# One decoder layer with expert retrieval: GpSimd takes part in the one-hot batches, the last table store goes in three parts, and the first group's roots are multiplied in behind its projections

## What is computed

```python
xn = rmsnorm(h, norm_mix_g);  proj = xn @ w_in               # 2048 columns: a | b | c | v
ya = rmsnorm(pool_mixer(a), norm_a_g)                        # windows 2, 4, 8, 16, then a 128x128 map
yb = rmsnorm(b * causal_conv3(c * v), norm_b_g)
h  = (h + concat(ya, yb) @ w_out)[16:]
xf = rmsnorm(h, norm_ffn_g)
s  = (xf @ w_query) . sub_keys                               # 8 heads, 2 halves, 128 keys each
top 16 of each half -> 256 sums -> top 16 -> expert = 128*i1 + i2, gates = softmax
out = h + sum over 8*16 experts of gate * gelu(u_e . xf) * v_e;  out = rmsnorm(out) * g
```

## Time and profile before

| | us |
|---|---|
| median of 3 runs | 2589.92 |
| the profiled execution, its own time | 2585.36 |
| its span | 2583.3 |
| PE busy | 2485.5 (96%) |
| DVE busy | 1967.7 (76%) |
| POOL busy | 1438.9 (56%) |
| ACT busy | 430.4 (17%) |
| mean granted clock of PE | 0.988 |

### The profile page before, as it was taken

One profiled execution on the slowest core, in us unless ns is written; L12 is line 12 of the kernel. 1 busy time (PEld: TensorE's weight loads), 2 busy tenths in 40 slices (PEclk: granted clock), 3 DMA queues, 4 the chain that ended last, 5 costly groups with the idle time before them and its releaser, 6 DMA issues.

```text
span 2583.3 us, 23989 instructions
## 1 busy us (share of the span) xinstructions
PE 2485.5 (96%) x7573; PEld 1367.0 (53%) x7573; DVE 1967.7 (76%) x4240; ACT 430.4 (17%) x793; POOL 1438.9 (56%) x1169
## 2 busy tenths in 40 slices
PE   8999999999788899999999999999999999999998
PEld 6687785877666344444444444444444444444443
DVE  3308888788699779676888868778787777979788
ACT  1213313213787000010020000000000000000001
POOL 0000387587611257556666757666676766767664
PEclk9999999999999999999999999999999999999999
DMA  7553885865678889969999999999999999999997
GB/s 291 220 185 142 306 302 148 347 207 132 204 229 240 340 317 373 399 244 418 371 394 390 389 405 371 410 378 414 414 386 419 360 397 413 405 420 403 419 405 275
DMA packets 288061, 857.67 MB, mean 332 GB/s; under 512 B 42048, under 2 KB 99392, under 8 KB 273344
## 3 DMA queue, kind: packets, MB, share of 16 engines
q0 software_dynamic: 167184, 541.73, 55.4%
q1 hardware_dynamic: 108400, 289.25, 29.5%
q10 hardware_dynamic: 12352, 25.17, 2.6%
HBM read 807.75 MB, written 48.30 MB: 331 GB/s over the span
## 4 chain that ended last, share of the span: by engine, by line
PE 70%; POOL 8%; DMA 8%; DVE 5%; issue 4%; ACT 3%; DVEq 1%; ACTq 0%; SPq 0%
PE pairs L820 27%; PE pairs L774 27%; PE pairs L684 9%; DMA ring<-in_expert_u,idx 6%; POOL gate_tables L635 5%; POOL ring L664 4%; PE pairs L731 2%; PE pairs L706 2%; ACT arena L972 1%; PE pairs L787 1%; DVE junk L1173 1%; ACT pick_all L853 1%; DMA arena<-gate_tables 1%; DMA arena<-in_w_all 1%; ACT arena L996 1%
## 5 line engine op out<-in xcount | busy, mean ns | idle before, releaser
L664 POOL DMA_INDIRECT ring<-in_expert_u,idx x512 | 645.1, 1260 | 644.0 <-DVE dots L1173 391.1
L820 PE MATMUL pairs<-arena 128*128 128x512 f32 x2048 | 887.3, 595 | 14.7 <-DVE arena L1239 8.5
L774 PE MATMUL pairs<-arena 128*128 128x512 f32 x2048 | 882.5, 592 | 0.0
L1173 DVE CUSTOM_DVE_ANT_0 junk<-ring,xf 128x1024 bf16<-128x1024 f32 x512 | 612.8, 1223 | 196.0 <-DMA ring<-in_expert_u,idx 192.2
L664 POOL DMA_INDIRECT ring<-in_expert_v,idx x512 | 576.8, 1127 | 293.5 <-DVE arena L1184 134.1
L820 PEld LDWEIGHTS pairs<-arena 128*128 128x128 f32 x2048 | 390.4, 191 | 509.1 <-issue 501.3
L774 PEld LDWEIGHTS pairs<-arena 128*128 128x128 f32 x2048 | 388.6, 190 | 486.5 <-issue 486.5
L1184 DVE SCALAR_TENSOR_TENSOR arena<-ring,arena 128x1024 f32<-128x1024 f32 x381 | 474.3, 1281 | 107.5 <-DMA ring<-in_expert_v,idx 106.4
L684 PE MATMUL pairs<-arena 128*128 128x256 f32 (+1 forms) x1792 | 397.4, 385 | 9.0 <-ACT arena L927 5.3
L684 PEld LDWEIGHTS pairs<-arena 128*128 128x128 f32 x1792 | 344.0, 192 | 60.4 <-ACT arena L927 5.9
L980 ACT ACTIVATE arena<-pairs 128x512 f32<-128x512 f32 x128 | 76.3, 597 | 1177.5 <-PE pairs L774 1159.9
(11 more groups left out here) (169 smaller groups left out, 1093.8 us busy)
## 6 DMA issues: line engine op xcount, KB each, us to landing
arena<-in_w_all SPq DMA_DIRECT2D x80, 1024.0 KB, 6.4
arena<-in_uT SPq DMA_DIRECT2D x128, 512.0 KB, 7.8
arena<-in_expert_v SPq DMA_DIRECT2D x128, 512.0 KB, 9.6
arena<-gate_tables SPq DMA_DIRECT2D x32, 1024.0 KB, 9.1
gate_tables<-arena SPq DMA_DIRECT2D x11, 2048.0 KB, 9.7
gate_tables<-junk ACTq DMA_DIRECT2D x4, 2048.0 KB, 15.1
ring<-in_expert_u,idx POOLq DMA_INDIRECT x512, 9.2
ring<-in_expert_v,idx POOLq DMA_INDIRECT x512, 8.8
```

The costliest lines, as they stand in the source:

```text
L664: nc.gpsimd.indirect_dma_start(out=ring[:, r % RING, :], out_offset=None, in_=expert_u if table == "u" else expert_v, in_offset=bass.Indir ...
L774: last = nc.tensor.matmul(score_bank[x], uslot[:, x % USLOTS, k * P:(k + 1) * P], xfT[:, k, :], start=(k == 0), stop=(k == KD - 1))
L820: last = nc.tensor.matmul(o_bank[n % 4], gated[:, x % GSLOTS, t * P:(t + 1) * P], vrows[:, j, half * 512:(half + 1) * 512], start=(j == 0) ...
L1173: nc.vector.tensor_tensor_reduce(out=junk[:, r % 2, :], in0=row, in1=xf[:, t % 2, :], scale=1.0, scalar=0.0, op0=ALU.mult, op1=ALU.add, ac ...
```

## The change

The first group's columns are multiplied by the gain alone, ahead of everything (`tensor_scalar`, in place). `pa` step 0 runs ahead of `sumsq`. The squares are added up on DVE first (`add_x(0)`), so that `sumsq` has two matmuls in place of eight. The reciprocal root, kept in `work` and not in `std`, is multiplied in when DVE evicts the ten `pa` and `bcv` steps of group 0 (`scaled`); ACT evicts none of these.

In the batches, ACT makes the first one-hots of batch 1 and of batches 2, 6, 10, ... (13), DVE those of 0, 4, 8, ... (12), and POOL those of 3, 5, 7, ..., 47 (23), by eight `tensor_scalar` of 128x128 each. In POOL's queue they stand ahead of the gather that follows the row used by batch b-3 plus the ring: batch 3 ahead of the gather of row 72, batches 5 and 7 ahead of row 73, and so on. The last store is in three parts, and the gates 1 wait for the second part and no longer for the whole.

`FILL` has a new place y2 between `add_y` and `roots_y`, and other figures. By the planner, 28 and 29 rows are used in the two queries, 27 and 28 before, and the scatters stand behind the gathers of rows 35 and 64.

```diff
-        for gate, y, outp, query in ((0.0, 0.0, 0.0, 0.0), (4.0, 22.0, 10.0, 68.0), (4.0, 22.0, 10.0, 68.0), (0.0, 15.0, 0.0, 66.0))]
+        for gate, y, y2, outp, query in ((0.0, 0.0, 0.0, 0.0, 0.0), (4.0, 13.0, 6.0, 10.0, 70.0), (4.0, 13.0, 6.0, 10.0, 70.0), (0.0, 10.0, 3.0, 0.0, 66.0))]
...
-    steps = [("sumsq", 0, 0)] + [("pa", 0, i) for i in range(4)]
+    steps = [("pa", 0, 0), ("sumsq", 0, 0)] + [("pa", 0, i) for i in range(1, 4)]
...
+    evictor = [{"outp": "dve", "ynorm": "roots"}.get(kind, "dve" if n == 0 and kind in ("pa", "bcv") else "act") for kind, n, _ in steps]
...
+                    "gate": ("bcv", n, 5), "y": ("pool", n, 0) if n < GRPS - 1 else ("turn", n, GT - 1), "y2": ("outp", n, GT - 1), "outp": ("ynorm", n, 0)}[where]
...
+        BY_ACT = [b for b in range(BATCHES) if b == 1 or b % 4 == 2]
+        BY_POOL = [b for b in range(BATCHES) if b % 2 == 1 and b > 1]
+        rows_then = [rows + sum(len(plan["hots", c]) for c in range(b + 1)) - sum(len(plan["hots", c]) for c in range(BATCHES)) for b in range(BATCHES)]
+        hots_before = {}
+        for b in BY_POOL:
+            hots_before.setdefault(rows_then[b - 3] + RING, []).append(b)
...
-                    sp.dma_start(to[:, 2:], of[:, 2:]).then_inc(table_kept[c % STAGES], 16)
+                    sp.dma_start(to[:, 2:HALF_GROUPS // 2], of[:, 2:HALF_GROUPS // 2]).then_inc(next_kept, 16)
+                    sp.dma_start(to[:, HALF_GROUPS // 2:], of[:, HALF_GROUPS // 2:]).then_inc(table_kept[c % STAGES], 16)
...
+            sp.wait_ge(next_kept, 16)
+            load_gates(1)
             stage_kept(last_stage)
-            load_gates(1)
...
+            def first_hots(b):
+                c = b % HOTBUFS
+                pool.wait_ge(table_full, 2 * (b - HOTBUFS) + 2)
+                if b // (P // HOTS) > 0:
+                    pool.wait_ge(turned_out, b // (P // HOTS))
+                for t in range(HOTS):
+                    k = b * HOTS + t
+                    last = nc.gpsimd.tensor_scalar(hots[:, c, 0, t, :], iota[:], routeT[:, 0, k:k + 1], None, ALU.is_equal)
+                last.then_inc(hot_pool, 1)
...
+                    for b in hots_before.get(r, ()):
+                        first_hots(b)
...
-                if b % 2 == 1:
-                    pe.wait_ge(hot_first, b // 2 + 1)
+                if b in BY_ACT:
+                    pe.wait_ge(hot_act, BY_ACT.index(b) + 1)
+                elif b in BY_POOL:
+                    pe.wait_ge(hot_pool, BY_POOL.index(b) + 1)
...
+            def scaled(kind, i):
+                step = (kind, 0, i)
+                dve.wait_ge(pe_step, full(step))
+                pair = psum[:, position[step] % PAIRS, :]
+                if kind == "pa":
+                    nc.vector.tensor_tensor(abuf[0][:, i, :], pair[:, 0:COLS], root_x(0), ALU.mult).then_inc(dve_emptied, 1)
+                else:
+                    halves = pair.rearrange("p (c t) -> p c t", c=2)[:, :, 0:COLS]
+                    nc.vector.tensor_tensor(projb[:, 2 * i:2 * i + 2, :], halves, root_x(0).unsqueeze(1).to_broadcast([P, 2, COLS]), ALU.mult).then_inc(dve_emptied, 1)
+                dve.drain()
...
+            for s in range(2):
+                dve.wait_ge(x_squared, s + 1)
+                for k in range(NG * s, NG * s + NG):
+                    nc.vector.tensor_scalar(xnT[0][:, k, :], xnT[0][:, k, :], g_mix[:, k:k + 1], None, ALU.mult).then_inc(xn_ready, 1)
+            add_x(0)
             norm_x(0)
...
                 fill(n, "y")
                 add_y(n)
+                fill(n, "y2")
                 roots_y(n)
...
-                if b % 2 == 0:
+                if b % 4 == 0:
                     nc.vector.tensor_tensor(hots[:, c, 0], iota[:].unsqueeze(1).to_broadcast([P, HOTS, KEYS]),
```

65 lines of the change are left out of this document (39 added, 26 removed).

## The result

| | before | after |
|---|---|---|
| median of 4 runs, us | 2587.39 (2581.70 to 2595.16) | 2615.03 (2610.87 to 2619.73) |
| span of the profiled execution, us | 2583.3 | 2613.3 |
| mean granted clock | 0.988 | 0.980 |

The kernel after takes 1.0108 times as long, 95% interval 1.0087 to 1.013: **slower by 28 us**, where 2578.4 us, 11.5 us faster, had been forecast.

The account below looks back on a forecast made before the run. DVE was taken as the fullest engine in the batches, ACT next; PE is full from 1218 us. Batches 9.0 (including the start and y norm), store 1.0 and late stretch 1.5 sum to 11.5 us: 2578.4 us, range 2565 to 2602.

Parts of the forecast that it names:

- Part 3: One-hot batches: POOL comparisons of 0.3 us, eight batches in 24.1 instead of 26.44 us, batches ending 9.0 us earlier.
- POOL instructions over 0.6 us: One-hot batches: a sign that the forecast is wrong, as these alone make POOL the bound; no size given.
- variants of 0.5 us: One-hot batches: POOL comparisons arrive late, 25.5 us for eight batches, 4 us gained in all, 2586 us; chance 0.16.
- The slow clock: One-hot batches: an allowance of 0.7 us in the forecast end of the batches.
- The pace itself: One-hot batches: DVE's 22.2 us plus 0.06 us per POOL instruction make 24.1 us for eight, 3.01 a batch.
- Rival (b): One-hot batches: each POOL comparison holds DVE's next for its whole length, 31.5 us for eight, 2619.5 us; chance 0.12.
- Part 1: The start: "pa" ends at 28.6 instead of 34.0 us, 5.4 us gained.
- Part 2: Norm of y: 3.5 us gained in groups 1 and 2, 6.3 us later in group 3, scatters delayed 2 us.
- Part 4: Last store in three: gates(1) issued earlier, 1 us gained; two rows fewer in the late stretch, 1.5 us.
- two rows fewer in the late stretch: Late stretch: fewer remaining rows gain 1.5 us, between 0 and the 5.9 us that PE lacks there.

Follow-up runs that it names:

- Run 16: The kernel after, with POOL's one-hots only from batch 13 on and a fourth one-hot buffer from batch 12 on: 2584.89 us.
- run 7: The kernel after, with POOL's one-hots only from batch 9 on and four of eight comparisons made per POOL batch: 2571.38 us, ratio 0.9945 to the kernel before.
- run 4: The kernel after with DVE and ACT making all first one-hots as before, and POOL's 184 comparisons going to a place nobody reads: 2586.87 us.
- run 8: The kernel before plus the new start alone, with POOL making two of DVE's four batches in eight, none of ACT's: ratio 0.9986 to the kernel before.
- run 5: The kernel after, with POOL's one-hots only from batch 9 on, earlier batches dealt as in the kernel before: 2596.98 us, ratio 1.0042 to the kernel before.
- run 11: The kernel after, POOL from batch 9 on, using two 128x1024 instructions (subtraction, comparison) with a drain between instead of eight short ones: 2623.00 us.
- run 12: The kernel before with only the last store in three parts and the gates 1 waiting for the second: ratio 0.9996 to the kernel before.

## Why the prediction was wrong, point by point

**Part 3, POOL's comparison: the step that failed.** The prediction took 0.3 us each from an affine_select on 128x128, the nearest row it had the earlier trace rows. The comparison takes 0.59 us at least and 0.70 at the mean; and for the time that POOL stands in a cycle, 3.9 us, most of it waiting for a buffer, the sum had no term. Both ends of the bound that was drawn, 0 and 0.29 us, were for what POOL takes from DVE; for the instruction's own length there was one value and no upper end. The prediction did write that "POOL instructions over 0.6 us" alone make POOL the bound, but gave that case no price and its variants of 0.5 us 0.16 of a chance. With the length now measured the case comes to 32 x 0.70 + 3 x 1.06 = 25.6 us of POOL in eight batches. That alone would still be less than the 26.44 us before: the price by itself takes the gain, and the waiting on top of it makes the loss.

The sum against the trace: batch 3 at 696.64 instead of 690.1 us, 6.5 us (4.4 from the scatters, 2.3 from eight longer comparisons, -0.2 from the gathers); then 45 batches at (863.31 - 696.64) / 45 = 3.70 instead of 3.01 us, 31 us. Together they are the 37.7 us between the forecast end of the batches, 825.6, and the real one. Of the 31 us some 9 are POOL's work (25.7 us a cycle instead of 24.1) and 22 its waits and gaps (29.6 less 25.7 us a cycle, over 45 batches). The slow clock, for which the prediction had 0.7 us in all, made PE's work 2.1 us longer in each cycle; how much of that reaches the time isn't separated. Run 16 had nearly the same clock and a cycle of 27.05 us, so most of the waiting isn't the clock's.

**The pace itself.** 24.1 us for eight batches was right for the price assumed (run 7: 24.1 and 24.2 in the middle cycles), partly by luck in how work and waits share it. What POOL takes from DVE was forecast as 0.06 us for each of POOL's instructions and measured as 0.075 (run 4). But the reading behind it, that DVE's 24.50 us made the cycle of the kernel before and ACT was "the next", was wrong: relieving DVE of two batches in eight moved nothing (run 8). An engine's busy time alone doesn't say who holds a cycle; who is waited for between the tiles does, and that was ACT.

**Three buffers.** The prediction named POOL's queue ahead of batch 3 but not the room. A batch's buffer comes free when PE is through with the one three before, so POOL has two batches, some 6 us, for 4.7 to 5.6 us of comparisons and perhaps a gather, and while PE does its score tile POOL runs out of room. Run 16 gave back 2.8 us a cycle at the mean (27.05 against 29.84 in run 5) by one buffer alone. At the price of run 7 the room was enough: the two errors count together.

**Rival (b)** came nearest, 2619.5 us against 2615.0, by a mechanism that run 4 excludes for these comparisons: right in size by luck. Its other direction is real. A stretch of POOL's comparisons in the kernel after, listed from three of their starts, and DVE beside them:

```profile
745.23 9.16 POOL L672 TENSOR_SCALAR arena<-iota,arena 128x128 f32<-128x128 f32 x13
745.81 8.58 POOL L672 TENSOR_SCALAR arena<-iota,arena 128x128 f32<-128x128 f32 x12
...
747.26 7.13 POOL L672 TENSOR_SCALAR arena<-iota,arena 128x128 f32<-128x128 f32 x11
```
```profile
745.60 1.21 DVE L1205 CUSTOM_DVE_ANT_0 junk<-ring,xf 128x1024 bf16<-128x1024 f32 x1
```

They start every 0.58 us, but the one from 745.81 lasts to 747.26: DVE's instruction with two inputs runs from 745.60 to 746.81, and POOL's ends 0.45 us behind it. That is the rule of the Trainium skill ("SBUF — State Buffer", Who interferes with whom) that a VectorE instruction with two inputs and a GpSimd instruction that reads exclude each other. The trace agrees for POOL as the one that waits: of the 184 comparisons the 156 beside which no instruction of DVE with two inputs ran took 0.59 to 0.69 us, and all 18 of more than 0.70 us had one beside them. The full block in the other direction, of which the prediction made 31.5 us a cycle, doesn't show for the short comparisons (0.075 us each); run 11 shows it for a subtraction of 1.92 us.

**Part 1.** Forecast was an end of "pa" at 28.6 us, measured 27.97. The failed term is the one it was compared with: the old start's 34.01 us held a slow clock that the prediction took for a part of every first stretch, and that was an accident of one execution. Against the 30.06 of run 12 the new start gains 2 us, not 5.4 or 6.0. That 28.6 came out so near is in part luck: its 17.8 us held that slow stretch, and the new "pa" has a slow one of its own, 6.70 us for the first 16 instructions and 11.16 for the other 48.

**Part 2.** The direction was right at each place: no PE wait before the norm in groups 1 and 2; the pick in group 3 moved ahead of the root. Group 2's queries had begun 7.4 us earlier (443.94 instead of 451.29), group 3's only 1.0 (596.45 instead of 597.48), so group 3 cost 6.3 us, as forecast. The scatters started 6.6 us earlier, at 515.34 (6.9 forecast), and ended 2.5 us earlier, at 682.98 (678.6 forecast): 80 of them took 167.6 us, before 163.6. Over all traces this chain took 162.8 to 167.9 us with the old fill (mean 164.5 of 12) and 164.6 to 167.6 with the new one (mean 166.5 of 8), so about half of the 4 us may be chance; what makes it long or short stays open.

**Part 4.** gates(1) went out 14.9 us behind the start of the tiles instead of 18.3, and PE's wait was 6.64 us instead of 8.10: 1.5 us, forecast 1. In run 12 it was nothing. The 1.5 us for two rows fewer in the late stretch didn't show: there PE waited 3.2 us for DVE's product with the gates (at 2124.33 and 2552.85), and before not at all. It wasn't the gates that were late: DVE waits for their loads in no trace after 1250 us. At 2552.85 the product stands in DVE's list behind four expert rows, and DVE waits for such rows' DMAs again and again (98.9 us in 95 waits after 1250 us for one kind of them alone). Of the 20 traces 15 have such waits of PE, 0.9 to 5.7 us in all: 9 of the 10 with the store in three, 6 of the 10 with the old one. They stay open.

## What to carry to other kernels

Before giving work to an engine that has little of it, price its instruction from both sides, not only what it takes from others: GpSimd's short operations can cost twice those of VectorE, and the case in which it becomes the bound needs a price and a chance of its own. Add its waits for room to its work: an engine with 25.7 us of work made a cycle of 29.6. To find who holds a cycle, read whom the main engine waits for between the fixed points, and which engine goes without a pause there; the highest busy share can belong to a bystander, and work taken from the right engine at the wrong place of its order only lengthens its next wait. A helper needs lead: count how many buffers ahead it may begin, and give it batches far enough apart.

## What the runs showed of the hardware

- A comparison of 128x128 f32 with a scalar for each partition took GpSimd 0.59 us, and VectorE, with two operations in it, 0.33 to 0.34 (0.26 from start to start). With 64 columns GpSimd took 0.43 us at least, with 1024 columns 2.81 us at the median; a subtraction with two inputs of 1024 took 1.92 us, less than the comparison with one.
- GpSimd waits out VectorE's instructions with two inputs: single comparisons of up to 2.54 us in the kernel after, beside two such instructions in a row. VectorE loses 0.075 us to each of GpSimd's short comparisons (run 4), but is held for the whole of GpSimd's subtraction with two inputs of 1024: a comparison of 0.33 us lasts 1.9 to 2.6 us (x_wide, all 20 times).
- Between its two wide instructions, with a drain between them, GpSimd stood for 2.3 us at the mean, 0.17 at the least and 5.60 at the most (x_wide). VectorE was busy all the while; whether that is the cause is open.
- The same code reached the end of the batches at 834.57 us in one execution and at 825.29 in another, 9 us apart, with 4 of them from the first 34 us, where the granted clock differed. A difference of a few microseconds between two single profiles isn't one between two kernels.
